# A two-block transformer kernel on one core: the first two up tiles of the MLP woven together, and the residual's loop on VectorE put in another order

## The reference, cut to what matters

```python
def rms_norm(x, g):
    xf = x.astype(jnp.float32)
    y = xf * lax.rsqrt(jnp.mean(xf * xf, axis=-1, keepdims=True) + RMS_EPS)
    return (y * g.astype(jnp.float32)).astype(x.dtype)

def second_block(x, ...):
    ...
        x = x + cat @ w_out[l]
        h = rms_norm(x, norm_mlp[l])
        x = x + jnp.square(jax.nn.relu(h @ w_up[l])) @ w_down[l]
    return x
```

## Time and profile before

| | |
|---|---|
| time, median of 3 runs | 1225.06 us (1225.05 to 1227.48) |
| the profiled execution | 1218.84 us |
| its span | 1217.0 us |
| TensorE busy | 1145.2 us (94%) |
| VectorE busy | 630.0 us (52%) |
| ScalarE busy | 423.5 us (35%) |
| GpSimd busy | 492.7 us (40%) |
| mean granted TensorE clock | 0.954 of full speed |

### The profile page before, as it was taken

One profiled execution on the slowest core, in us unless ns is written; L12 is line 12 of the kernel. 1 busy time (PEld: TensorE's weight loads), 2 busy tenths in 40 slices (PEclk: granted clock), 3 DMA queues, 4 the chain that ended last, 5 costly groups with the idle time before them and its releaser, 6 DMA issues.

```text
span 1217.0 us, 16005 instructions
## 1 busy us (share of the span) xinstructions
PE 1145.2 (94%) x5777; PEld 970.3 (80%) x5777; DVE 630.0 (52%) x1121; ACT 423.5 (35%) x847; POOL 492.7 (40%) x489
## 2 busy tenths in 40 slices
PE   6999999999999989998987778999899999999998
PEld 5888888888788878897876777687688888888887
DVE  6869777685666728319437676435541231231321
ACT  5373587263365512132246654321130110110110
POOL 0000000000623329799860000005876776777772
PEclk9999999999999999998999887579899999999999
DMA  6322323323210103333330000001323232332321
GB/s 250 125 85 90 103 87 104 121 81 111 86 36 19 36 1 121 104 122 114 112 104 1 1 2 1 0 1 52 122 87 104 87 104 91 99 101 88 103 86 52
DMA packets 27277, 97.15 MB, mean 80 GB/s; under 512 B 3024, under 2 KB 3408, under 8 KB 27088
## 3 DMA queue, kind: packets, MB, share of 16 engines
q1 hardware_dynamic: 27216, 96.32, 23.9%
HBM read 94.21 MB, written 2.10 MB: 79 GB/s over the span
## 4 chain that ended last, share of the span: by engine, by line
PE 65%; issue 19%; DVE 9%; ACT 4%; POOL 1%; DMA 1%; SPq 0%; DVEq 0%; POOLq 0%; ACTq 0%
PE bank L1100 20%; PE bank L1102 20%; PE bank L1101 20%; PE bank L745 2%; PE bank L782 1%; DVE arena L1734 1%; PE bank L762 1%; DVE arena L1806 1%; DVE wl L1757 1%; ACT wh L1444 1%; ACT xh L1432 1%; DMA x<-x_in 1%; POOL wl L505 0%; DVE arena L1835 0%; DVE xl L1726 0%
## 5 line engine op out<-in xcount | busy, mean ns | idle before, releaser
L501 POOL TENSOR_TENSOR hold<-hold 128x2 f32<-128x2 f32 x117 | 28.2, 241 | 651.1 <-PE bank L1102 651.1
L1100 PE MATMUL bank<-xh,wh 128*128 128x512 f32 x568 | 226.8, 399 | 17.3 <-DVE xl L1726 15.1
L1101 PE MATMUL bank<-xl,wh 128*128 128x512 f32 x568 | 222.4, 392 | 0.0
L1102 PE MATMUL bank<-xh,wl 128*128 128x512 f32 x568 | 222.3, 391 | 0.0
L1100 PE MATMUL bank<-yh,wh 128*128 128x512 f32 x520 | 204.6, 393 | 7.0 <-POOL wl L505 4.9
L1101 PE MATMUL bank<-yl,wh 128*128 128x512 f32 x520 | 203.6, 392 | 0.0
L1102 PE MATMUL bank<-yh,wl 128*128 128x512 f32 x520 | 203.6, 392 | 0.0
L505 POOL TENSOR_TENSOR wl<-raw,wh 128x512 fp32r<-128x512 f32 x117 | 175.8, 1502 | 0.0
L504 POOL TENSOR_TENSOR wl<-raw,wh 128x512 fp32r<-128x512 f32 x117 | 158.0, 1351 | 9.8
L1100 PEld LDWEIGHTS bank<-xh,wh 128*128 128x128 f32 x568 | 107.5, 189 | 41.3 <-issue 11.3
L502 POOL TENSOR_SCALAR wh<-raw 128x1024 fp32r<-128x1024 f32 x117 | 125.8, 1076 | 0.0
(11 more groups left out here) (241 smaller groups left out, 1805.3 us busy)
## 6 DMA issues: line engine op xcount, KB each, us to landing
raw<-weight_units SPq DMA_DIRECT2D x173, 512.0 KB, 3.4
x<-x_in SPq DMA_DIRECT2D x4, 512.0 KB, 7.8
out_fm<-x SPq DMA_DIRECT2D x8, 256.0 KB, 2.0
arena<-tables SPq DMA_DIRECT2D x1, 1024.0 KB, 9.9
par<-params SPq DMA_DIRECT2D x1, 166.0 KB, 2.3
arena<-swa_table SPq DMA_DIRECT2D x1, 128.0 KB, 10.8
ident<-identity SPq DMA_DIRECT2D x1, 64.0 KB, 7.7
```

The costliest lines, as they stand in the source:

```text
L501: pool.tensor_tensor(hold[:], hold[:], hold[:], ALU.add).then_inc(held, 1)
L1100: pe.matmul(out, lh, rh, start=start, stop=False)
L1101: pe.matmul(out, lh, rl, start=False, stop=False)
L1102: return pe.matmul(out, ll, rh, start=False, stop=stop)
```

## The change

On TensorE the new function `first_two` multiplies row tiles 0 to 6 of up tile 0, then row tiles 0 to 6 of up tile 1, then row tile 7 of up tile 0 and of up tile 1. The sum of squares moves from behind up tile 1 to behind up tile 2, the spread of `rstd` from behind up tile 3 to behind up tile 4. On VectorE the addition of tile m+1 goes ahead of the low part of tile m, and the seven additions of squares go behind all eight low parts.

```diff
+            def first_two():
+
+                for ks in (range(KD - 1), range(KD - 1, KD)):
+                    for i in range(2):
+                        if ks[0] == 0:
+                            pe.wait_ge(x_new, 2 * KD + i + 1)
+                        feature_major(U_MLP + i, (U_MLP + i) % RING, up_bank(i, True), xh, xl, ks=ks,
+                                      ready=(xl_ready, 4 * KD + 1, 1) if i == 0 else None)
+
             def mlp_chunk(c, first, later):
-                for i in range(KD):
+                if first:
+                    first_two()
+                for i in range(2 if first else 0, KD):
...
-                    feature_major(U_MLP + 16 * c + i, (U_MLP + i) % RING, up_bank(i, first), xh, xl,
-                                  ready=(xl_ready, 4 * KD + 1, 1) if first and i == 0 else None)
-                    if first and i == 1:
+                    feature_major(U_MLP + 16 * c + i, (U_MLP + i) % RING, up_bank(i, first), xh, xl)
+                    if first and i == 2:
                         pe.wait_ge(x_new, 3 * KD)
                         sum_squares(3, B[4])
-                    if first and i == 3:
+                    if first and i == 4:
                         spread_rstd(3, B[5])
...
+            for m in range(KD + 1):
+                if m < KD:
+                    wait_done(dve, ("out2", m))
+                    dve.tensor_tensor(x[:, m, :], B[m][:], x[:, m, :], ALU.add).then_inc(x_new, 1)
+                if m > 0:
+                    dve.wait_ge(x_new, 2 * KD + m)
+                    low_part(m - 1, xh, xl, "g_mlp", 4 * KD + m)
             for m in range(KD):
-                wait_done(dve, ("out2", m))
-                dve.tensor_tensor(x[:, m, :], B[m][:], x[:, m, :], ALU.add).then_inc(x_new, 1)
-                dve.wait_ge(x_new, 2 * KD + m + 1)
-                low_part(m, xh, xl, "g_mlp", 4 * KD + m + 1)
                 add_square(3, m)
             token_norm(3, B[4])
```

## The result

The changed kernel took 1217.1 us (median of 4 runs, 1214.55 to 1218.98), the kernel before 1226.1 us in the same comparison (4 runs): ratio 0.9924, 95% interval 0.9905 to 0.9943, so 9.0 us less. Applied to the 1225.06 us of the runs shown that is 1215.7 us.

A forecast was written before the change was run, and what follows sets the result against it. VectorE's residual loop was taken as the bound from about 856 to 867 us, TensorE before and behind it. First two tiles 7.6, less squares 0.2 and relu chain 2.1, gave 5.3 us less: 1219.8 us, range 1216.8 to 1223.8.

The forecast's parts named there:

- The signs named ahead: Wrong if the first two up tiles still wait, squares end behind 873.5, or the chain's wait is over 3 us.
- The loop on VectorE is the bound from 856 us: Residual's loop, 4.54 us a turn, bounds the kernel from about 856 to 867 us; before and behind it TensorE does.
- 7.6 us from the first two tiles: Up tiles 0 and 1 on TensorE: neither row tile 6 nor 7 waits; they end at 866.95 against 874.57.
- GpSimd costs nothing: GpSimd's splits for up tiles 1 to 3: price 0, at worst 0.4 us twice.
- Squares 0.2 us: TensorE's wait for VectorE's seven additions of squares, ahead of the sum behind up tile 2: 0.2 us, range 0 to 0.9.
- the first rival: Clock falls behind the new relu-chain wait and squares are 0.9 us late: 2.9 us less, 1222.2 us; chance 0.27.
- The relu chain, 2.1 us: Later spread of rstd makes TensorE wait ahead of down tile 0's last row tile: 2.1 us, bounds 0 to 3.7.
- The clock: priced at 0 for this wait: TensorE's clock behind the relu-chain wait stays up: price 0, range 0 to 1.6 us.
- The sum.: All terms together: 7.6 - 0.2 - 2.1 = 5.3 us less; chance of this forecast 0.50.
- the range: Forecast time from 1216.8 to 1223.8 us, each end with 0.9 us for the runs' own spread of 2.4.
- the step from the sum to the median: 5.3 us less gives 1213.5 on the profiled execution; runs' median is 6.2 us above that, so 1219.8 us predicted.
- the best case of the mechanism (7.4 us less): Rival: relu chain doesn't bind, as VectorE's low parts miss GpSimd's splits: 7.4 us less, 1217.7 us; chance 0.06.

The follow-up runs named there:

- the squares in the gaps: Changed kernel with four of seven squares in VectorE's idle time between out2's tiles 4 to 7, sum and spread moved back; 0.9939 of the kernel before, twice.

## Why the prediction was right and wrong

- **The signs named ahead.** None of the three that would have shown me wrong came: the first two tiles don't wait, the squares end ahead of the sum, the chain's wait is under 3 us.
- **The loop on VectorE is the bound from 856 us: right.** With its order alone changed, TensorE has no wait on low parts; with the old order and woven tiles it still has one of 1.9 us.
- **7.6 us from the first two tiles: right.** The sum begins at +38.8 us now, behind one tile (5.45 us) more; before at +41.1. 41.1 - (38.8 - 5.45) = 7.7 us. Low part 7 ended at 866.1, +26.3 us; I had said 859.4 on the old trace, +25.9.
- **GpSimd costs nothing: right,** and not by much: the squares in the gaps made it late by half a microsecond.
- **Squares 0.2 us: they cost 0.** The 0.2 followed from no row: at 1.80 us each the seven would have ended at 872.0, ahead of the 872.4 at which they are asked for, so it was a guess inside 0 to 0.9. They took 10.52 us, 1.50 each. The row stands at +26.2 to +36.8 and is asked for at +38.8. The Trainium skill (SBUF — State Buffer, "SBUF: two separate sides") has it that a VectorE instruction with two SBUF inputs and a GpSimd instruction that reads SBUF exclude each other for the whole instruction. By that rule I had estimated 2.0 us a square and a wait of 0.9, and the first rival had taken the 0.9 over. The packed row shows 1.50 us beside an unbroken GpSimd: slower than the 0.69 alone, but less than strict turns with instructions of 1.3 us would give; the measurement decides.
- **The relu chain, 2.1 us: right mechanism, too dear.** From the spread at 890.45 to the end of low part 7 at 913.08 + 0.69 = 913.77 it took 23.3 us. I had worked out 23.7 to 24.2, taking up to 1.2 us for the last low part, which in fact took 0.69, and then put 2.1 in the sum, near the upper end of 1.7 to 2.2. The wait was 1.24 us, and its restart some 0.3.
- **The clock: priced at 0 for this wait, and it stayed at 1.00, by luck.** My reason was that the wait would be nearer to 2.03 us, behind which the clock had stayed, than to 2.43, behind which it fell. With TensorE's order only it fell behind 1.87 us, so the length doesn't decide and the reason doesn't hold.
- **The sum.** 7.7 - 0 - 1.5 = 6.2 us in the trace, against 7.6 - 0.2 - 2.1 = 5.3. The terms were off by 0.9 us together, two thirds of it the relu chain: that is the term of the sum that was mis-sized, 2.1 us for a measured 1.5. With all terms right the forecast would have been 1218.9 us, inside the range, and the 1215.7 measured would still have been outside.
- **What failed: the step from the sum to the median, and the range.** I wrote that the median of the runs shown is 6.2 us above the profiled execution, took the difference over unchanged and allowed 0.9 us "for the runs' own spread of 2.4". Those three runs happened to lie close together. The timed executions of the same program spread over 11.8 us with a standard deviation of 3.0, which is 1.5 us for a mean of four. The range's lower end was the best case of the mechanism (7.4 us less) with only 0.9 us for the measurement, and 9.0 us less fell out of it. Of these 9.0, 6.2 are in the stretch, about 2 are the luck of four runs, and for the last 1 us the cause stays open. The 6.2 us between the profiled execution and the median were the sign that I read and did not use.

## What to carry to other kernels

When a producer's loop bounds a few consumers, take out of its turns what nobody waits for yet, and let the consumer do the ready part of two tiles before the last part of either; here each half alone was worth under 2 us and both 6, because each half alone left a wait, and in both cases a slow clock came with it. A step that is moved behind one more tile moves everything that hangs on it: work out the chain from it to its last user, and its slack, ahead of the move. Compare stretches between two instructions that both traces have, and ask how far executions of one program lie apart before giving a range.

## What the runs showed of the hardware

- **How long TensorE had stood still did not settle whether its clock fell.** Behind stalls of 2.43 us and 3.34 us (VectorE's order only) it fell, and so it did behind one of 1.87 us (TensorE's order only: 0.66), and with the spread one tile later among three short ones, 1.50, 1.53 and 1.09 us with three matmuls between them (0.66). Behind 2.03 us and 1.24 us (changed kernel) it stayed at 2.4 GHz.
- **A fall cost 2.8 us in one place and 1.6 in another** (VectorE's order only; the kernel before), by what TensorE had to do at 1.2 GHz: a large matmul took 0.43 us and not 0.23. I had one price for all.
- **Seven additions of squares in a row took 1.50 us each beside GpSimd's splits,** 1.77 with a low part between them and 0.69 with GpSimd idle (changed kernel; the earlier trace rows).
- **One program, one core, and 1216.0 to 1227.8 us.** The granted clock over the attention's stretches, 0.88 or 0.66 in the same 60 us, went with it.
